# First eight rows and first weight strip of the gated linear unit split inside the first projection; its first three blocks put ahead of the retention

## The reference, cut to what matters

```
h = rms_norm(x)                       # 2048 + 8 tokens, width 1024
z = h @ w_in0                         # 40 column strips of 128
q, k, v, g_a, u, g_b = split(z)
o_ret, s_ret = retention(rotary(q), rotary(k), v, s0)      # 4 heads, blocks of 128 tokens
a_out = head_group_norm(o_ret) * silu(g_a)
y5 = gelu(s5_scan(u))                 # diagonal state space, then GELU
y5 = y5 * sigmoid(y5 @ glu_w + glu_b) # the gated linear unit
b_out = y5 * silu(g_b)
x = x + concat(a_out, b_out) @ w_out0
```

## Time and profile before

| | us |
|---|---|
| median of 3 runs | 3227.0 |
| lowest, highest run | 3221.94, 3229.91 |
| profiled execution, its own time | 3224.71 |
| its span on the core | 3222.8 |

### The profile page before, as it was taken

The page is one execution under the profiler, slowest core; times in us unless marked ns, Lnnn a source line. Parts: engine busy times, 40 slices in busy tenths (PEclk is TensorE's granted clock), DMA queues, the critical chain, the costliest instruction groups (busy, mean ns, idle before and its releaser), DMA issues. The chain is left out here.

```text
span 3222.8 us, 45906 instructions
## 1 busy us (share of the span) xinstructions
PE 3050.9 (95%) x16972; PEld 2692.6 (84%) x16972; DVE 1510.5 (47%) x2888; ACT 1043.6 (32%) x1751; POOL 1082.6 (34%) x680
## 2 busy tenths in 40 slices
PE   6999899799999879899999989999999999997999
PEld 6999899688888679786788859999988888886886
DVE  7999344404540088886422212133345444545542
ACT  4111122312221055543211110034545443455751
POOL 2222222122222256561121202244434433454441
PEclk8999999899999979998999989999999989998899
DMA  5433655455653365555523322343344333333333
GB/s 139 105 120 120 194 176 156 123 110 169 180 153 97 92 236 197 200 197 201 195 103 125 118 107 80 92 157 96 122 123 133 108 126 105 128 118 126 121 126 119
DMA packets 377212, 442.86 MB, mean 137 GB/s; under 512 B 46264, under 2 KB 315192, under 8 KB 367856
## 3 DMA queue, kind: packets, MB, share of 16 engines
q1 hardware_dynamic: 278672, 373.05, 36.8%
q10 hardware_dynamic: 98400, 67.91, 6.8%
HBM read 285.26 MB, written 159.81 MB: 138 GB/s over the span
## 5 line engine op out<-in xcount | busy, mean ns | idle before, releaser
L803 PE MATMUL p_psum<-p_h_hi,p_w_hi 128*128 128x344 f32 (+1 forms) x1600 | 563.6, 352 | 0.0
L803 PE MATMUL p_psum<-p_h_lo,p_w_hi 128*128 128x344 f32 (+1 forms) x1600 | 557.7, 349 | 0.0
L803 PE MATMUL p_psum<-p_h_hi,p_w_lo 128*128 128x344 f32 (+1 forms) x1600 | 557.4, 348 | 0.0
L2600 PE MATMUL p_psum<-p_h_hi,p_w_hi 128*128 128x344 f32 (+1 forms) x1248 | 448.8, 360 | 8.4 <-DVE p_h_lo L2321 3.4
L2600 PE MATMUL p_psum<-p_h_lo,p_w_hi 128*128 128x344 f32 (+1 forms) x1248 | 442.3, 354 | 0.0
L2600 PE MATMUL p_psum<-p_h_hi,p_w_lo 128*128 128x344 f32 (+1 forms) x1248 | 441.6, 354 | 0.0
L387 POOL CAST p_w_hi<-p_w_raw 128x1024 fp32r<-128x1024 f32 x80 | 89.9, 1124 | 804.9 <-PE p_psum L803 654.2
L803 PEld LDWEIGHTS p_psum<-p_h_hi,p_w_hi 128*128 128x128 f32 x1600 | 302.2, 189 | 34.0 <-issue 9.5
L803 PEld LDWEIGHTS p_psum<-p_h_hi,p_w_lo 128*128 128x128 f32 x1600 | 302.1, 189 | 25.3
L803 PEld LDWEIGHTS p_psum<-p_h_lo,p_w_hi 128*128 128x128 f32 x1600 | 302.1, 189 | 24.6
L2339 DVE COPY p_out<-p_psum 128x344 f32<-128x344 f32 (+1 forms) x156 | 90.7, 583 | 463.9 <-PE p_psum L2600 463.8
(11 more groups left out here) (351 smaller groups left out, 6061.0 us busy)
## 6 DMA issues: line engine op xcount, KB each, us to landing
p_w_raw<-in_w_in SPq DMA_DIRECT2D x144, 512.0 KB, 5.3
z<-p_out ACTq DMA_DIRECT2D x64, 512.0 KB, 3.5
z<-p_out SPq DMA_DIRECT2D x64, 512.0 KB, 3.2
p_raw<-z SPq DMA_DIRECT2D x32, 1024.0 KB, 5.5
rg_raw<-z SPq DMA_DIRECT2D x16, 1536.0 KB, 7.8
c_m_raw<-m SPq DMA_DIRECT2D x16, 1024.0 KB, 7.0
u_s<-p_out SPq DMA_DIRECT2D x128, 73.0 KB, 3.1
p_shared<-u_s SPq DMA_DIRECT2D x32, 292.0 KB, 5.4
```

What stands on the lines that cost most here:

```text
L803: ins = pe.matmul(bank, wv[par][:, k, :], h[hf][:, k, c0:c0 + n], start=(k == 0 and j == 0), stop=(k == KD - 1 and j == 2))
L2600: ins = pe.matmul(bank, wv[par][:, k, :], h[hf][:, k, c0:c0 + n], start=(k == 0 and j == 0), stop=(k == KD - 1 and j == 2))
```

## The change

The gated linear unit's inputs for the first half of the tokens and its weight strip 0 are prepared by `project_s5`. Their four buffers (`glu_side`) are laid out before `project_s5` begins, at the place where `retention_combine` expects them, so they stay. The second half's stretch of twelve strips (26 to 37) becomes three of four. Behind the last unit SP stores `h_last`, waits for the last unit's products and its landed stores, and loads the weight strip `gw_raw` and rows 0 to 2 into the room that the units used; behind strips 26 to 29 it loads rows 3 to 5, each behind the splitting of the row three before, and behind strips 30 to 33 rows 6 and 7. DVE does all the splitting (`split_row`) after its last unit: sixteen copies and sixteen subtractions for eight rows, and two instructions for the weights.

The wait for the last stores to `z` moves from ACT, ahead of the barrier, to SP, behind the load of tile 0. In `retention_combine` PE starts with all three blocks of strip 0 (block 2 in bank 1, which the turned outputs use later, so step 2 waits for that block's sigmoid), and turns tile 0 after them. The loads of rows and strip 0 weights, ACT's rounding, DVE's remainders and POOL's splitting of strip 0 go away there; ACT takes the three sigmoids of strip 0 together.

```diff
-             ((0, 2, None), (2, 6, None), (8, 2, None), (10, 16, "unit"), (26, 12, None), (38, 2, None)))
+             ((0, 2, None), (2, 6, None), (8, 2, None), (10, 16, "unit"), (26, 4, None), (30, 4, None), (34, 4, None),
+              (38, 2, None)))
+ROWS_AT = {"unit": (0, 1, 2), 26: (3, 4, 5), 30: (6, 7)}
...
+def row_parts(stage, hf):
+
+    stage = stage.rearrange("p (t c) -> p t c", c=YCH)
+    views = [(0, HALF, L8, stage[:, :, 0:CHH].rearrange("p t c -> p c t"))]
+    if hf == 0:
+        views.append((HALF, COLS[0], 1, stage[:, 0:1, CHH + 1:YCH].rearrange("p t c -> p c t")))
+    return views
...
+def glu_side(nc, ctx, made):
+
+    ctx.enter_context(nc.sbuf_tensor("rg_pad" if made else "rg_gap", [P, 24], F32, side="right"))
+    if not made:
+        return [ctx.enter_context(nc.sbuf_tensor(f"rg_{n}", shape, F32R, side="right")) for n, shape in (
+            ("h_hi", [P, KD, COLS[0]]), ("h_lo", [P, KD, COLS[0]]), ("w_hi0", [P, KD, P]), ("w_lo0", [P, KD, P]))]
...
-def project_s5(nc, a, x_in, z, y_dram, out_p, out_s):
+def project_s5(nc, a, x_in, z, y_dram, out_p, out_s, stored, glu):
...
+        y_hi, y_lo = by_half(glu[0])[0], by_half(glu[1])[0]
+        gw_hi, gw_lo = glu[2], glu[3]
...
+        y_row = [room[:, e * L8 * YCH:(e + 1) * L8 * YCH] for e in range(3)]
+        gw_raw = room[:, 3 * L8 * YCH:3 * L8 * YCH + D].rearrange("p (k c) -> p k c", c=P)
...
                 strips(1, s0, n, job)
-            sp.wait_ge(hs_done, 2 * NU + 1)
-            sp.dma_start(out_p, h_last[:]).then_inc(out_st, 16)
+                if job == "unit":
+                    sp.wait_ge(hs_done, 2 * NU + 1)
+                    sp.dma_start(out_p, h_last[:]).then_inc(out_st, 16)
+                    sp.wait_ge(y_mm, 2 * NU + 2)
+                    for par in range(2):
+                        sp.wait_ge(y_st[par], 64 * NU + CREDIT)
+                    sp.dma_start(gw_raw, a["glu_w"][0]).then_inc(gw_ld, 16)
+                for r in ROWS_AT.get(job or s0, ()):
+                    if r >= 3:
+                        sp.wait_ge(y_lo_done, r - 2)
+                    sp.dma_start(y_row[r % 3], y_dram[0, r * P:(r + 1) * P, :, :].rearrange("p t c -> p (t c)"))\
+                        .then_inc(y_ld[r % 3], 16)
             sp.wait_ge(out_st, 32)
-            for par in range(2):
-                sp.wait_ge(y_st[par], 64 * NU + CREDIT)
...
-            for par in range(2):
-                act.wait_ge(stored[par], stores_before(1, N_P0 - 2 + par) + 16)
...
+            def split_row(r):
+                dve.wait_ge(y_ld[r % 3], 16 * (r // 3 + 1))
+                for c0, c1, l, v in row_parts(y_row[r % 3], 0):
+                    ins = dve.tensor_copy(y_hi[:, r, c0:c1].rearrange("p (c t) -> p c t", t=l), v)
+                ins.then_inc(y_hi_done, 1)
+                dve.wait_ge(y_hi_done, r + 1)
+                for c0, c1, l, v in row_parts(y_row[r % 3], 0):
+                    ins = dve.tensor_tensor(y_lo[:, r, c0:c1].rearrange("p (c t) -> p c t", t=l), v,
+                                            y_hi[:, r, c0:c1].bitcast(F32).rearrange("p (c t) -> p c t", t=l),
+                                            ALU.subtract)
+                ins.then_inc(y_lo_done, 1)
+
+            dve.wait_ge(y_mm, 2 * NU + 2)
+            for par in range(2):
+                dve.wait_ge(y_st[par], 64 * NU + CREDIT)
+            dve.wait_ge(out_st, 32)
+            dve.wait_ge(gw_ld, 16)
+            dve.tensor_copy(gw_hi[:], gw_raw).then_inc(gw_hi_done, 1)
+            dve.wait_ge(gw_hi_done, 1)
+            dve.tensor_tensor(gw_lo[:], gw_raw, gw_hi[:].bitcast(F32), ALU.subtract).then_inc(gw_lo_done, 1)
+            for r in range(KD):
+                split_row(r)
...
-def retention_combine(nc, a, z, y_dram, mix, out_p, out_s, w_out, x_in, x_out, norm_w):
+def retention_combine(nc, a, z, y_dram, mix, out_p, out_s, w_out, x_in, x_out, norm_w, sem, z_stored,
+                      glu):
...
-        h_hi, h_lo = (by_half(right(n, [P, KD, COLS[0]], F32R)) for n in ("h_hi", "h_lo"))
-        w_hi0, w_lo0, w_hi1 = (right(n, [P, KD, P], F32R) for n in ("w_hi0", "w_lo0", "w_hi1"))
+        h_hi, h_lo = by_half(glu[0]), by_half(glu[1])
+        w_hi0, w_lo0 = glu[2], glu[3]
+        right("held", [P, 2 * KD * (COLS[0] + P)])
...
-            return 6 + block_no(g, b) % 2
+            return 1 if block_no(g, b) == 2 else 6 + block_no(g, b) % 2
...
             load(0)
-            load_strip(0)
-            load_row(0, 0)
-            load_row(0, 1)
+            for par in range(2):
+                sp.wait_ge(z_stored[par], stores_before(1, N_P0 - 2 + par) + 16)
             for d, s in ((q_decay, "q_decay"), (k_decay, "k_decay"), (mask, "ret_mask"), (gn_w, "gn_w"), (eye8, "eye8")):
                 sp.dma_start(d[:], a[s]).then_inc(const_ld, 16)
+            load(1)
+            load_strip(1)
             sp.dma_start(bias[:], a["glu_b"]).then_inc(bias_ld, 16)
-            load_row(0, 2)
-            load_row(0, 3)
-            load(1)
             load_gate(0)
-            for r in range(4, KD):
-                load_row(0, r)
-            load_strip(1)
             load_gate(1)
...
-            split(0)
+            pool.sem_inc(w_hi_done, 1)
+            pool.sem_inc(w_ld[0], 16)
...
-            for r in range(4):
-                high(0, r)
+            act.sem_inc(y_hi_done, 2 * KD)
+            for i in range(4):
+                act.sem_inc(y_ld[i], 32)
             take_v(0, P)
             silu(0, P)
-            for r in range(4, KD):
-                high(0, r)
             act.wait_ge(bias_ld, 16)
             strip_gate(0)
...
-                if g % KD:
+                if g != KD:
                     sigmoid(g, 0)
+                if g == 0:
+                    sigmoid(0, 1)
+                    sigmoid(0, 2)
...
+            dve.sem_inc(y_lo_done, KD)
             turn(0, P)
-            for r in range(2):
-                low(0, r)
             dve.wait_ge(const_ld, 16 * N_CONST)
             decay_keys(0)
             mask_scores(0)
-            for r in range(2, KD):
-                low(0, r)
+            pre(0)
...
+            pe.sem_inc(w_lo_done, 1)
+            pe.wait_ge(w_lo_done, 1)
+            first_blocks(0)
+            strip_block(0, 2)
             pe.wait_ge(ident_ld, 16)
             turn_v(0, P)
...
+                if k == 2:
+                    pe.wait_ge(ev_done, block_no(1, 0))
                 if k >= 2:
                     turn_o(k - 2, 0)
-                if k == 1:
-                    first_blocks(g)
...
-                if half_of(g) == 0 and g != LAST_A:
+                if g and half_of(g) == 0 and g != LAST_A:
                     strip_block(g, 2)
                 new_states(k - 1)
```

More of the change, by code:

```diff
@@ L2768, in scratch @@
         return nc.dram_tensor(name, shape, F32, kind="Internal").ap()
+    joint = ExitStack()
+    sem = joint.enter_context(semaphores(nc, "rg"))
+    z_stored = [sem(f"z_stored{i}") for i in range(2)]
+    with ExitStack() as ahead:
+        glu = glu_side(nc, ahead, False)
     z0 = {"z": scratch("z0", [NT, P, 32, P]), "zs": scratch("z0s", [P, 32, NS])}
```

41 lines of the change are left out of this document (21 added, 20 removed).

## The result

| | kernel before | changed kernel |
|---|---|---|
| median of 5 runs each, us | 3229.5 | 3210.3 |
| lowest, highest | 3221.9, 3232.8 | 3209.7, 3216.0 |
| ratio of the times, 95% interval | | 0.9949, 0.9934 to 0.9965 |
| profiled execution, span | 3222.8 | 3211.6 |

The change made the kernel faster by 19 us at the median, where 30 were forecast; 3210.3 lies outside the range of 3190 to 3205.

What follows compares the result with a forecast made beforehand. It took PE's waiting and half-speed clock between first projection and retention's step 2 as the time to win. 32.2 - 2.0 - 0 = 30.2 us off a 3227.0 median gave 3197, range 3190 to 3205.

Steps and rivals of the forecast that it cites:

- The barrier: Between projection and retention: moving the wait for z stores to SP gains 2.8 us, bounds 0 and 2.8.
- The 72 matmuls: Strip 0's blocks, first on PE: released by DVE's memset, 11.3 plus 3.0 us, hidden while tile 0 comes in.
- POOL's five steps: Between POOL's rotations of tiles 0 and 1: back to back in 11.9 us, so step 2 starts at 1144.6, 32.2 earlier.
- PE's own way: PE's work from tile 0's rotation to step 2: some 11 us, to about 1143, shorter than POOL's.
- the signs that the prediction named: Trace checks, including tile 1's k turned at 1142 to 1148 and POOL back to back between the two rotations.
- The rule that I weighed against the change: DVE and POOL share a port pair; one holds it for a whole instruction while the other fully blocks.
- Step 2: Retention's second step: loses 2.0 us for the clock's return and tile 1's keys behind tile 0's norm; bounds 0 and 3.0.
- The last strips: Loads and splitting moved into the projection's end cost 0, strip 28's weights ready 0.9 us early; bounds 0 and 4.5.
- The second rival: Strip 28 starved: DVE's row splitting holds POOL off, 14 us late, time 3214, or 3205 with half; chance 0.08.
- the third: Slower than before: strip 32's weights queue behind late loads of rows 3 to 5, time 3237; chance 0.03.
- From step 3 on: Later retention steps: order as before, where PE had no gap, so nothing takes the gain back.
- The first rival: PE stays at 1.2 GHz in the thin work after the 72 matmuls, time 3201 to 3205; chance 0.13.

Runs made afterwards that it cites:

- after: The changed kernel itself, unedited, in its first profiled execution (span 3211.6 us); median of 5 runs 3210.3 us, ratio 0.9949 to the kernel before.
- wait_alone: Kernel before with only the wait for the last z stores moved from ACT to SP behind tile 0's load; one run, 3223.9 us.
- blocks_late: Changed kernel with PE's earlier order: strip 0's three blocks stand behind tile 0's scores; median 3217.6 us, ratio 0.9962 to the kernel before.
- serial: Changed kernel with one more wait: DVE starts strip 0's gate instructions only after POOL has split strip 1's weights; one run, 3208.7 us.
- lean: Changed kernel with strip 0's sum moved ahead of tile 0's sines and tile 1's keys ahead of tile 0's norm on DVE; median 3203.2, repeated 3206.0 us.
- after_again: The changed kernel run again without any edit; median 3205.5 us, ratio 0.9928 to the kernel before.
- after_third: The changed kernel run a third time without any edit; median 3207.9 us, ratio 0.9937 to the kernel before.
- lean_act: lean with strip 1's weight conversion on ACT instead of POOL, and strip 0's product behind tile 1's sines on DVE; median 3209.1 us, ratio 0.9934.
- turn_first: Changed kernel with strip 0's two gate instructions on DVE moved behind tile 1's sines; one run, 3215.5 us.

## Why the prediction was right and wrong

**The barrier** was right: SP's first instruction came 1.64 behind the store's issue (1117.12 and 1118.76 in the trace of after), 2.8 sooner, and wait_alone has the same with nothing else changed.

**The 72 matmuls** were right, and cheaper: 12.95 instead of 14.3, and DVE's memset does not release them, so they start 1.0 sooner. Neither matters, as tile 0's rotation ends 18.05 behind the last matmul (1132.17 + 2.34 - 1116.46) where 18.2 was predicted (1132.7 - 1114.46). The order itself is worth 9.2, less than the 14.3 that I wrote for the missing cover. In blocks_late the turning comes only 6.1 later than in the changed kernel, since PE there doesn't wait for POOL ahead of it, as it does here for 5.49.

**POOL's five steps** are the step that failed. I took 11.9 from a stretch of steady running and got 15.9, from 1134.51 to 1150.38. Of the 4.0 more, 2.46 are waiting for DVE's sines and 1.8 the slower splitting (5.26 instead of 3.44), less 0.3 in the other steps. The sum treated POOL as a chain of its own; but its last step needs tile 1's sines from DVE, and DVE has strip 0's sum and product ahead of them. In the earlier trace rows the sines were done at 1188.05, 3.4 ahead of POOL's rotation, so the wait didn't show there. It showed in the handover of the kernel before, where the same two instructions already stood ahead of the sines:

```profile
1162.47 1.23 DVE L1443 TENSOR_TENSOR rg_out<-rg_h_hi,rg_h_lo 128x1032 f32<-128x1032 f32 x1
1163.74 1.23 DVE L1448 TENSOR_TENSOR rg_zg<-rg_zg,rg_out 128x1032 f32<-128x1032 f32 x1
1165.01 2.45 DVE L1394 TENSOR_TENSOR rg_cross<-rg_raw,rg_rope 64x1024 f32<-64x1024 f32 x2
```

```profile
1167.61 2.36 POOL L1185 TENSOR_TENSOR rg_rot<-rg_rot,rg_cross 128x1024 f32<-128x1024 f32 x1 [5.19 <-DVE rg_cross L1394]
```

The change took the remainders of rows away ahead of these instructions, but left their order. Turned behind the projection: 33.8 on the mean of three, 28.7 earlier than before, where 32.2 was predicted. PE's own way to that point came out as worked out: it ended at 1144.95 (1143 in the prediction, and the projection ends 2.0 later). Two of the signs that the prediction named failed with POOL's steps: POOL was not back to back, and the turning at 1150.44 lies outside 1142 to 1148, also if the 2.0 are taken off.

The rule that I weighed against the change was used for the wrong place. The Trainium skill, page "SBUF — State Buffer", section "SBUF: two separate sides", says that of GpSimd and a DVE instruction with two inputs in SBUF, whichever starts first has the shared ports for its whole instruction while the other fully blocks. The traces agree with it in the handover: 5.86 us of work of the two engines, each by itself in serial (1.05, 2.35, 1.23 and 1.23), took 6.6 side by side, from 1138.71 to 1145.32, with the last 1.3 of POOL's gate among them. I asked only whether this could starve strip 28, and it did not.

**Step 2** was to lose 2.0, with bounds 0 and 3.0, as the return of the clock. It lost 3.9 (14.53 less 10.67, the same in all three profiles): 2.27 of it is the wait for the keys, which I had seen standing behind tile 0's norm, and priced with the clock's figure instead of with DVE's queue. The clock took most of the rest: at 0.90 over 14.53 it lacks 1.45. lean takes the wait away, and its step 2 is 12.6 long, 1.9 more than before.

**The last strips** came out as worked out in the changed kernel, narrowly. Waits of PE in the changed kernel from 955 to 1200, all of them:

```profile
PE rg_psum L1667 <- POOL rg_rot L1235: 7.0, 2, 5.5
PE rg_psum L1674 <- DVE rg_k_nat L1513: 3.4, 3, 2.3
PE rg_psum L1708 <- DVEq L1541: 2.6, 1, 2.6
```

None is in the projection. POOL in the changed kernel at strip 28:

```profile
979.50 1.62 POOL L423 CAST p_w_hi<-p_w_raw 128x1024 fp32r<-128x1024 f32 x1 [13.57 <-DMA p_w_raw<-in_w_in]
981.21 4.28 POOL L425 TENSOR_TENSOR p_w_lo<-p_w_raw,p_w_hi 128x1024 fp32r<-128x1024 f32 x1
986.07 1.50 POOL L423 CAST p_w_hi<-p_w_raw 128x1024 fp32r<-128x1024 f32 x1 [0.58 <-PE p_psum L860]
```

The split was done at 985.49, and PE's end of strip 27 released the next conversion at 986.07: 0.58 to spare, where the prediction had 0.9; in after_again and after_third it was 0.72 and 0.38. In two edited kernels, whose edits don't touch this place, it was too late: PE waits 1.41 (serial) and 1.57 (lean_act) for POOL's split ahead of strip 28, and in turn_first 0.73 at the same place, which its trace puts down to ACT. So the cost of 0 holds for the three executions of the changed kernel and has hardly any margin. The second rival in its own size (POOL kept out until DVE's queue is empty, 14 late) is refuted, and so is the third: no wait for strip 32.

**From step 3 on** almost nothing is taken back. Tile 2's outputs follow tile 1's after 20.15 instead of 19.60, 0.3 of it a wait for keys, so that 24.3 of the 24.9 are left; from there on the steps are as long as before. To layer 1 it is 732.6 to 734.9 before and 733.0 to 735.7 after. The first rival, PE at 1.2 GHz, had the right place for two of the losses (scores of tile 0 took 1.98 and v of tile 1 1.91, against 1.16 and 1.04 in step 2), but PE waited for POOL behind them anyway.

**The sum.** The stretch gave 24.9 in place of 30.2: 5.3 missing, 3.5 of it in POOL's steps and the rest in step 2. These two steps alone would have left 3202. The level was off too: the three runs that I had gave 3227.0, 44 give a mean of 3229.0. And 24.9 in the stretch are 20.4 in the times. Of these 4.5, step 3 has 0.6; where the other 3.9 go isn't settled: the three profiles have the projection's end 1.7 later and layer 1 7.1 longer in the mean, but single executions differ by more than that. 3197 + 5.3 + 2.0 + 4.5 is 3208.8, and 16 runs have a mean of 3208.6. So the queues explain 5.3 of the 13.3 by which 3197 missed the median. The range could have been better without any of this: the lower bound of my own sum was a gain of 20, 3207, and I cut it at 3205 since the rivals seemed unlikely (3210.3 lies outside 3207 as well); and three runs over 8 us don't give a level to 2.

## What to carry to other kernels

When waiting ahead of a stretch goes, add up the queue of every engine that feeds its next step, not of the one that released it before: here DVE stood one link behind POOL, and a wait of POOL for DVE, 5.19 long, stood in the trace of before. Where DVE and POOL work at the same time on tiles in SBUF, count their times one behind the other, as they came here, unless a row shows overlap. Compare single profiles only over the stretch that was changed, and take the level from many runs: 10 us of 1300 came and went here with no edit.

## What the runs showed of the hardware

DVE and POOL alternate: side by side POOL's conversion of 128x1024 took 2.04 and its subtraction 3.22 (alone 1.05 and 2.35), DVE's sum 2.42 (alone 1.23), and one of two equal DVE products 3.26 while the other took 1.22. Each of five instructions in a row ended its own lone duration, less 0.14 to 0.16, behind the end of the other engine's instruction, and in the handover the overlap won 1.3 us of some 8.

The same work was granted different clocks: 261 matmuls of layer 1, with PE busy all the time, had 0.87 and 0.96 in two executions of the changed kernel and 1.00 in one of the kernel before, and layer 1 took 1303.9 to 1313.7 us in one program. PE had worked without a pause for 40 us ahead of the pieces with 0.87 and 1.00, at 0.96 in both; what decides is not visible in these traces.

A barrier between two stages took 1.58 and 1.64 us here from ACT's last store issue to SP's first instruction; a store that must land first made it 4.46.
